# Two transformer blocks on one core: the last mixer by pairs of heads, another order of its projections, and other fillings of the pauses

## The chip, the core and the metric

The kernel runs on one of the eight cores of a Trainium2 chip. Five engines work side by side and meet at semaphores: TensorE (PE, matrix products), VectorE (DVE), ScalarE (ACT), GpSimd (POOL) and SyncE (SP, which issues the transfers here). The metric is device time in microseconds; lower is better. Three runs of the kernel before took 1088.26, 1089.15 and 1089.99 us.

## The reference, cut to what matters

One sequence of 256 tokens of width 1024 goes through three layers: a first block (gated delta rule and attention as mixer 1, then an MLP) and two layers of a second block: mixer 2 (differential attention) with MLP, and mixer 3 (stick-breaking attention) with MLP. Everything is float32. The change is about mixer 3:

```python
def stick_breaking_attention(h, w_q, w_o, k, v):      # 16 heads of 64
    q = (h @ w_q).reshape(b, s, B_HEADS, B_HEAD_DIM).transpose(0, 2, 1, 3)
    def block(args):
        qb, start = args
        z = jnp.einsum('bhqd,bhkd->bhqk', qb, k).astype(f32) * scale
        mask = kpos[None, :] < qpos[:, None]
        log_beta = jax.nn.log_sigmoid(z)
        log_1m = jnp.where(mask, jax.nn.log_sigmoid(-z), 0.0)
        between = lax.cumsum(log_1m, axis=3, reverse=True) - log_1m
        a = jnp.where(mask, jnp.exp(log_beta + between), 0.0)
        return jnp.einsum('bhqk,bhkd->bqhd', a.astype(v.dtype), v)
    ...
    return o @ w_o
# around it, for each layer: x = x + rms_norm(mixer(rms_norm(x))), x = x + rms_norm(swiglu(rms_norm(x)))
```

k and v come from `rms_norm(x) @ kv_w` with a gain of their own.

## The kernel before, in words

**Weights.** All weights stream through the same path. `raws` lists them in the order of use; each is one transfer of 1 MB into one of three `RAW` buffers and two "halves" of 128x1024. ACT copies a half, rounded, to `WH` (L1393) and DVE subtracts to get the rest, `WL` (L1839); in mixer 3 every other subtraction is POOL's (L2419). A product of float32 quality is then three matmuls, high by high, low by high, high by low (`mm3`, L653 to L655). A half lies in one of eight slots: slots 0 to 3 are `WH`/`WL`, slots 4 to 7 are `SPARE`, a region that overlaps the scratch of the mixers and so belongs to the MLPs alone. `ahead(n)` in ACT's, DVE's and POOL's programs prepares all halves up to n+3, and a half waits until PE is done with the one that held its slot before.

**Order.** Nothing is scheduled at run time. Each engine runs its own program in order, and `in_order` makes all of them follow the same written list of steps (`STAGE_4` for mixer 3), each engine taking from it the steps that it has a function for. Each entry below is a step: `p.j` is projection half j, 24 in all, in the order of `S_ORDER` (v, k and q, four pieces each, two halves a piece); `o.i` multiplies by half i of the output weight.

**Mixer 3 before.** Step `s.h` of head h has three parts on PE. For h-4 it forms the sums (`b_sums`): two products of a triangle of ones and one of a full square of ones with the softplus of the scores, which gives the reverse cumulative sum, 128x256, 128x128 and 128x128 (L1365 to L1367). For h it forms the scores (`b_score`), keys by queries, with 64 rows of the array (L1354, L1355: 256 and 128 columns, since the mask leaves out a quarter). For h-6 it forms the values (`b_values`), whose output is 64 partitions high (L1377, L1378). Even heads use rows or columns 0 to 63 of the array, odd heads 64 to 127. All of these operands are plain float32, and each of these matmuls runs as two passes. Between them DVE scales and masks (L2381), ACT takes the absolute value and the exponential, then for four heads at once (`l.p`) the logarithm, DVE completes the softplus (L2389), adds the sums (L2376), and ACT takes the last exponential. The buffers ZM and LS hold eight heads of 128x384 each. The values of a pair of heads go to `MH`/`ML` as soon as the last key or value projection has read these (until then to `OT`), since the projections of k and v read their input there, and those of q read `UH`/`UL`.

**Output.** Steps o.0 to o.5 add one half of the output weight each to four tiles of 128x512 in PSUM. `out_last` (o.6) takes the last two halves tile by tile, so that tile (0,0) ends first.

**Between stages.** `between(r)` is the work of ACT, DVE and POOL from the finished sums to the next input: squares (`sq`), gain (`mx`), root on POOL (`r0`, `r1`), addition to H (`ad`), squares of H (`hs`), scaling (`xn`, L1855), then 16 pieces of features (`fe`), each transposed by PE (L687), scaled by ACT and DVE. r = 1, 3, 5 stand behind the three mixers, 2, 4, 6 behind the three MLPs. PE waits in `entry(r)`: it runs `WARM[r]` dummy products first (`keep_warm`, L664), then four transposes, then transposes and first products in turn. After mixer 1 (`BETWEEN_FIRST`) the preparation of the MLP's halves is spread over this work (`hi.k`, `lo.k`); after mixers 2 and 3 it all stands before or behind it.

## Time and profile before

| | us |
|---|---|
| median of three runs | 1089.15 (1088.26 to 1089.99) |
| the profiled execution, its own time | 1094.96 |
| span in it, first to last instruction | 1093.1 |
| PE busy | 1048.6 (96%) |
| PE weight loads busy | 953.5 (87%) |
| DVE busy | 637.7 (58%) |
| ACT busy | 563.2 (52%) |
| POOL busy | 85.2 (8%) |

All times in views are microseconds from the start of the span. Matmuls are pipelined, so the ends of PE's rows are modelled; the distance from the start of one row to the start of the next is what a piece of work takes on PE, and the text uses that. An idle time and what ended it stand in brackets behind a row. PEclk is the granted clock, 1.00 being 2.4 GHz. Mixer 3 runs from about 747 to 891, the last MLP from 903 to 1083.

### The profile page before, as it was taken

What the parts mean: (1) busy time and instruction counts of PE and PEld (TensorE: products, weight loads), DVE (VectorE), ACT (ScalarE), POOL (GpSimd) and SP (SyncE); (2) the same over time, 40 slices, a digit from 0 to 9 for tenths busy, and PEclk for the clock granted to TensorE, in tenths of its full rate; (3) what the DMA queues carried; (4) which work ended last, traced back from release to release, by engine and by line L of the source; (5) the groups of instructions that cost most, each with busy time, mean ns of one, the idle gap of its engine ahead of it and who ended that gap; (6) DMA issues with size and microseconds to landing.
All of it is one profiled execution on the core that took longest, in us unless ns stands there. A gap on an engine that the chain in (4) does not pass through costs nothing.

```text
span 1093.1 us, 17642 instructions
## 1 busy us (share of the span) xinstructions
PE 1048.6 (96%) x7367; PEld 953.5 (87%) x7367; DVE 637.7 (58%) x984; ACT 563.2 (52%) x1009; POOL 85.2 (8%) x84
## 2 busy tenths in 40 slices
PE   6999899999999999999899999998999999999997
PEld 5989887889999887988789999997999879999996
DVE  4797644587464557677875545548344566454553
ACT  5662354466453546556464434437676656343442
POOL 3012010110000001000100000000322210000000
PEclk9999899999999999999999999999999999999999
DMA  8323111074556454433346556464433334654641
GB/s 263 116 78 93 62 40 40 1 229 152 198 168 216 157 213 152 155 116 117 116 136 231 173 174 228 143 207 136 155 116 117 116 103 155 225 172 175 226 145 54
DMA packets 114974, 160.34 MB, mean 147 GB/s; under 512 B 3776, under 2 KB 99264, under 8 KB 114896
## 3 DMA queue, kind: packets, MB, share of 16 engines
q1 hardware_dynamic: 114896, 159.22, 43.8%
q8 instruction: 58, 0.95, 0.4%
q14 instruction: 20, 0.16, 0.0%
HBM read 158.16 MB, written 1.05 MB: 146 GB/s over the span
## 4 chain that ended last, share of the span: by engine, by line
PE 83%; DVE 9%; ACT 4%; issue 2%; POOL 1%; DMA 0%; SPq 0%; DVEq 0%; POOLq 0%; ACTq 0%
PE PS L653 23%; PE PS L655 22%; PE PS L654 22%; ACT SCR L1393 2%; DVE WL L1839 2%; PE PS L982 1%; PE PS L1354 1%; POOL SM L2423 1%; PE PS L687 1%; DVE SPARE L1839 1%; PE PS L1377 1%; PE PS L1275 1%; PE PS L977 1%; PE PS L1365 1%; DVE H L1875 1%
## 5 line engine op out<-in xcount | busy, mean ns | idle before, releaser
L1839 DVE TENSOR_TENSOR WL<-RAW,WH 128x1024 fp32r<-128x1024 f32 (+1 forms) x177 | 213.9, 1234 | 71.6 <-ACT WH L1393 71.4
L1393 ACT ACTIVATE WH<-RAW 128x1024 fp32r<-128x1024 f32 (+1 forms) x191 | 195.1, 1049 | 46.6 <-DMA RAW<-in_gu 28.9
L653 PE MATMUL PS<-UH,WH 128*128 128x256 f32 (+2 forms) x680 | 195.7, 288 | 3.9 <-DVE WL L1839 3.0
L655 PE MATMUL PS<-UH,WL 128*128 128x256 f32 (+2 forms) x680 | 194.4, 286 | 0.0
L654 PE MATMUL PS<-UL,WH 128*128 128x256 f32 (+2 forms) x680 | 194.4, 286 | 0.0
L1393 ACT ACTIVATE SCR<-PS 128x512 f32<-128x512 f32 (+7 forms) x233 | 100.7, 468 | 171.2 <-PE PS L655 118.9
L653 PEld LDWEIGHTS PS<-UH,WH 128*128 128x128 f32 (+1 forms) x680 | 129.8, 191 | 6.4 <-DVE WL L1839 3.7
L1839 DVE TENSOR_TENSOR SPARE<-RAW,SPARE 128x1024 fp32r<-128x1024 f32 x100 | 118.0, 1219 | 22.1 <-ACT SPARE L1393 22.1
L654 PEld LDWEIGHTS PS<-UL,WH 128*128 128x128 f32 (+1 forms) x680 | 129.3, 190 | 1.1
L655 PEld LDWEIGHTS PS<-UH,WL 128*128 128x128 f32 (+1 forms) x680 | 129.8, 191 | 0.5
L1937 DVE TENSOR_TENSOR SCR<-SCR,PS 128x512 f32<-128x512 f32 x34 | 23.4, 687 | 159.4 <-PE PS L655 108.2
L1393 ACT ACTIVATE SPARE<-RAW 128x1024 fp32r<-128x1024 f32 x100 | 100.3, 1048 | 27.3 <-DMA RAW<-in_gu 20.7
L653 PE MATMUL PS<-WH,MH 128*128 128x512 f32 (+1 forms) x288 | 108.3, 376 | 2.4 <-DVE ML L2395 1.2
L654 PE MATMUL PS<-UL,SPARE 128*128 128x256 f32 x384 | 108.2, 282 | 0.0
L653 PE MATMUL PS<-UH,SPARE 128*128 128x256 f32 x384 | 108.1, 281 | 0.0
L655 PE MATMUL PS<-UH,SPARE 128*128 128x256 f32 x384 | 107.6, 280 | 0.0
L654 PE MATMUL PS<-WL,MH 128*128 128x512 f32 (+1 forms) x288 | 105.4, 366 | 0.0
L655 PE MATMUL PS<-WH,ML 128*128 128x512 f32 (+1 forms) x288 | 105.3, 366 | 0.0
L2423 POOL TENSOR_TENSOR SM<-SM 128x1 f32<-128x1 f32 (+5 forms) x32 | 26.8, 840 | 778.4 <-DVE SM L1850 623.3
L1393 ACT ACTIVATE MH<-SCR 128x512 fp32r<-128x512 f32 (+1 forms) x37 | 22.6, 615 | 124.0 <-DVE SCR L1937 124.0
L653 PE MATMUL PS<-WH,UH 128*128 128x256 f32 (+2 forms) x264 | 80.9, 306 | 0.1
L654 PE MATMUL PS<-WL,UH 128*128 128x256 f32 (+2 forms) x264 | 76.5, 290 | 0.0
(307 smaller groups left out, 2093.2 us busy)
## 6 DMA issues: line engine op xcount, KB each, us to landing
RAW<-in_gu SPq DMA_DIRECT2D x44, 1024.0 KB, 5.3
RAW<-in_dn SPq DMA_DIRECT2D x22, 1024.0 KB, 7.2
RAW<-in_w_up SPq DMA_DIRECT2D x16, 1024.0 KB, 6.2
RAW<-in_w_down SPq DMA_DIRECT2D x16, 1024.0 KB, 5.0
RAW<-in_a_qkv SPq DMA_DIRECT2D x12, 1024.0 KB, 5.1
RAW<-in_w_in SPq DMA_DIRECT2D x11, 1024.0 KB, 5.3
RAW<-in_kv_w SPq DMA_DIRECT2D x8, 1024.0 KB, 5.6
RAW<-in_w_out SPq DMA_DIRECT2D x4, 1024.0 KB, 4.9
```

Source lines behind the costliest of these rows:

```text
L653: e.matmul(o, lh, rh, start=start, stop=False)
L654: e.matmul(o, lh, rl, start=False, stop=False)
L655: return e.matmul(o, ll, rh, start=False, stop=stop)
L687: e.transpose(PS[:, b, o:o + 128], XN[:, c, 128 * k:128 * k + 128], idn).then_inc(*turned.step((r, c, k)))
L977: ins = e.matmul(v[:, h, :], MT[:, h, :], X[:, h, :], start=True, stop=True)
L982: ins = e.matmul(v[:, h, :], XT[:, h, :], T0[:, h, :], start=True, stop=True)
L1275: ins = e.matmul(PS[:, 4 + i, 0:nk], QTT[64 * i:64 * i + 64, h, 128 * c:128 * c + 128], KTT[64 * i:64 * i + 64, h, 0:nk], start=True, stop ...
L1354: e.matmul(PS[:, b, 0:256], KTS[hp:hp + 64, j, 0:128], QTS[hp:hp + 64, j, :], start=True, stop=True)
L1393: return e.activation(o, i, func, bias=bias, scale=scale, accum_out=acc)
L1839: e.tensor_tensor(lo_of(n_), half_src(n_), hi_of(n_).bitcast(F32), SUB).then_inc(s_lo_dve, 1)
L1937: e.tensor_tensor(FB[:, g % 2, 1, :], FB[:, g % 2, 0, :], PS[:, ub + ((g - begun) * nb + nb - 1) % 4, :], MUL).then_inc(*f_2.step((r, g)))
L2423: e.tensor_tensor(o, x, s, POW).then_inc(*done)
```

## The change

It has four parts.

1. Mixer 3 works on pairs of heads q = 0 to 7. A step s.q makes the scores of both heads, head by head in turn, so that neighbouring matmuls lie in rows 0 to 63 and 64 to 127 of the array, in two PSUM banks. A new step c.q makes the sums of both heads (one matmul of 384 columns in place of 256 and 128, and one of 128), and a new step u.q the values of both, in columns 0 to 63 and 64 to 127 of the array and in the two halves of the partitions of one PSUM bank. The elementwise operations between are 128x768 instead of twice 128x384, and `l.p` (ACT) and the new `t.p` (DVE) take two pairs.
2. The projections come in another order: q1 before v1, q2 before v2, q3 before k3 and v3. The mixer's result goes to `UH`/`UL`, free once q3 is projected, instead of `MH`/`ML`. Four halves of the output weight instead of two are taken tile by tile at the end (`out_last`); steps o.4 and o.5 go.
3. The first MLP halves after mixers 2 and 3 lie in slots 4 to 7 first, as they did after mixer 1, and `BETWEEN_FIRST`, renamed `BETWEEN_MLP`, is used after all three mixers.
4. `WARM` changes, and three more dummies stand behind the first four transposes of every `entry`.

```diff
-S_ORDER = "v0 k0 q0 k1 v1 q1 k2 v2 q2 k3 v3 q3".split()
+S_ORDER = "v0 k0 q0 k1 q1 v1 k2 q2 v2 q3 k3 v3".split()
 STAGE_4 = steps_of(
-    "p.0 p.1 p.2 p.3 p.4 p.5 s.0 p.6 s.1 p.7 s.2 p.8 s.3 p.9 l.0 p.10 p.11 s.4 p.12 s.5 p.13 s.6 p.14 s.7 p.15 l.1 "
-    "p.16 p.17 s.8 p.18 s.9 p.19 s.10 p.20 s.11 p.21 l.2 p.22 os.0 p.23 s.12 os.1 o.0 s.13 o.1 s.14 o.2 s.15 o.3 l.3 "
-    "o.4 s.16 s.17 o.5 s.18 s.19 sv.14 sv.15 o.6")
+    "p.0 p.1 p.2 p.3 p.4 p.5 s.0 p.6 s.1 p.7 l.0 t.0 p.8 p.9 c.0 p.10 s.2 u.0 p.11 c.1 p.12 s.3 u.1 p.13 l.1 t.1 p.14 "
+    "c.2 p.15 s.4 u.2 p.16 c.3 p.17 s.5 u.3 p.18 l.2 t.2 p.19 p.20 c.4 p.21 s.6 u.4 os.0 p.22 s.7 os.1 p.23 p.24 c.5 l.3 "
+    "t.3 o.0 u.5 o.1 c.6 o.2 c.7 o.3 u.6 u.7 o.6")
-WARM = {0: 14, 1: 2, 2: 2, 3: 18, 4: 2, 5: 18}
+WARM = {0: 14, 1: 6, 2: 4, 3: 17, 4: 7, 5: 3}
...
-                head = (4, 5, 6, 7, 0, 1, 2, 3) if r == 2 else (0, 1, 4, 5, 2, 3, 6, 7, 4, 5)
+                head = (4, 5, 6, 7, 0, 1, 2, 3, 4, 5)[:8 + (b - a) % 8]
...
                 for k in range(4):
                     turn(0, k)
+                keep_warm(3, SUMS[r])
...
-                        out_last(r, [half_of(("out", r, 3), j) for j in range(2)], [6, 7], [mix_ready(r, 6), mix_ready(r, 7)])
+                        ks = range(4 if r == 5 else 6, 8)
+                        out_last(r, [half_of(("out", r, k // 2), k % 2) for k in ks], ks, [mix_ready(r, k) for k in ks])
...
+            def b_score(q):
+                ...
+                for kt in range(2):
+                    for i in range(2):
+                        hp = slice(64 * i, 64 * i + 64)
+                        ins = e.matmul(PS[:, i, 256 * kt:256 + 128 * kt], KTS[hp, q, 128 * kt:128 * kt + 128], QTS[hp, q, 128 * kt:],
+                                       start=True, stop=True)
+            def b_sums(q):
+                pe.wait_ge(*sh_sp[q])
+                for i in range(2):
+                    l = LS[q % 4][:, i, :]
+                    pe.wait_ge(*emptied[i])
+                    e.matmul(PS[:, i, 0:384], C["inclb"], l, start=True, stop=False)
+                    ins = e.matmul(PS[:, i, 128:256], C["ones"], l[:, 256:384], start=False, stop=True)
+            def b_values(q):
+                b, w = 2 + q % 2, LS[q % 4]
+                ...
+                for kt in range(2):
+                    for i in range(2):
+                        h = 2 * q + i
+                        ins = e.matmul(PS[64 * i:64 * i + 64, b, 128 * kt:256], VS[:, kt, 64 * h:64 * h + 64], w[:, i, 256 * kt:256 + 128 * kt],
+                                       start=kt == 0, stop=kt == 1)
...
-                in_order({1: BETWEEN_FIRST, 6: BETWEEN_LAST}.get(r, BETWEEN), dict(sq=sq, hs=hs, xn=xn, fe=fe, hi=next_halves))
+                in_order(BETWEEN_LAST if r == 6 else BETWEEN_MLP if r + 1 in MLP else BETWEEN, dict(sq=sq, hs=hs, xn=xn, fe=fe, hi=next_halves))
...
-                return lambda i: ahead(half_of(("out", r, i // 2), i % 2) if i < 6 else LAST_OUT[r] + 1)
+                return lambda i: ahead(half_of(("out", r, i // 2), i % 2) if i < 6 else LAST_OUT[r])
+                return lambda i: ahead(half_of(("out", r, i // 2), i % 2) if i < 6 else LAST_OUT[r] - 1)
```

In the last three lines the first is ACT's and DVE's before, the second ACT's now, the third DVE's now.

How the instructions move, at three places. (A row is line, operation, output and inputs, shape of the output; x2 means twice in a row.) First PE in the middle of mixer 3, where before every block between two projection halves holds the sums, scores and values of one head each:

```order
L1365 MATMUL PS<-SCR,CST 128x256
L1366 MATMUL PS<-SCR,CST 128x128
L1367 MATMUL PS<-SCR,CST 128x128
L1354 MATMUL PS<-SCR 128x256
L1355 MATMUL PS<-SCR 128x128
L1377 MATMUL PS<-SCR 64x256
L1378 MATMUL PS<-SCR 64x128
```

The same place of the changed kernel, a block of sums, then, 24 projection matmuls later, a block of scores and values:

```order
L1372 MATMUL PS<-SCR,CST 128x384
L1373 MATMUL PS<-SCR,CST 128x128
L1372 MATMUL PS<-SCR,CST 128x384
L1373 MATMUL PS<-SCR,CST 128x128
...
L1361 MATMUL PS<-SCR 128x256 x2
L1361 MATMUL PS<-SCR 128x128 x2
L1387 MATMUL PS<-SCR 64x256 x2
L1387 MATMUL PS<-SCR 64x128 x2
```

Scores and values of the two heads of a pair now stand next to each other, and the sums stand alone in their blocks.

Second, DVE at the end of mixer 3 and the start of the work behind it, before (L2376 adds the sums, L2395 and L2401 split the result, L1839 is a half's low part, L1869 `mx`, L1850 `r0` or `r1`, L1875 `ad`):

```order
L2376 SCALAR_TENSOR_TENSOR SCR<-PS,SCR 128x384 [waits s_bsum] x2
L2395 SCALAR_TENSOR_TENSOR ML<-PS,MH 128x256 [waits s_mix_hi] x2
L1839 TENSOR_TENSOR WL<-RAW,WH 128x1024 [waits s_hi]
L1839 TENSOR_TENSOR SPARE<-RAW,SPARE 128x1024 [waits s_hi] x2
L1869 SCALAR_TENSOR_TENSOR SCR<-PS,WROW 128x512 [waits s_wrow,s_mixsq0]
L1850 TENSOR_SCALAR SM<-SM 128x1 [waits s_mixsq0]
L1869 SCALAR_TENSOR_TENSOR SCR<-PS,WROW 128x512
L1875 SCALAR_TENSOR_TENSOR H<-SCR,SM,H 128x512 [waits s_mixed0,s_root0]
```

and now (the same operations are L2393, L2398, L1845, L1879, L1856 and L1885):

```order
L2393 SCALAR_TENSOR_TENSOR SCR<-PS,SCR 128x768 [waits s_bsum] x2
L1845 TENSOR_TENSOR WL<-RAW,WH 128x1024 [waits s_hi]
L2398 SCALAR_TENSOR_TENSOR UL<-PS,UH 128x256 [waits s_mix_hi] x2
L1845 TENSOR_TENSOR SPARE<-RAW,SPARE 128x1024 [waits s_hi] x2
L1879 SCALAR_TENSOR_TENSOR SCR<-PS,WROW 128x512 [waits s_wrow,s_mixsq0]
L1845 TENSOR_TENSOR SPARE<-RAW,SPARE 128x1024 [waits s_hi]
L1856 TENSOR_SCALAR SM<-SM 128x1 [waits s_mixsq0]
L1879 SCALAR_TENSOR_TENSOR SCR<-PS,WROW 128x512
L1885 SCALAR_TENSOR_TENSOR H<-SCR,SM,H 128x512 [waits s_mixed0,s_root0]
```

One subtraction for the next MLP has moved from before the first `mx` to behind it, ahead of `r0`.

Third, ACT around the second logarithm (SCR<-SCR,SM with the constant one as bias), now; before, its place had four operations of 128x384 and three projection halves before the next sums:

```order
L1402 ACTIVATE SCR<-SCR 128x768 [waits s_bz]
L1402 ACTIVATE SCR<-SCR 128x768 [waits s_bexp]
L1402 ACTIVATE SCR<-PS 128x256 [waits s_bvalue]
L1402 ACTIVATE WH<-RAW 128x1024 [waits s_raw0]
L1402 ACTIVATE SCR<-PS 128x256 [waits s_half]
L1402 ACT_TABLE_LOAD
L1402 ACTIVATE SCR<-SCR,SM 128x768
L1402 ACTIVATE SCR<-SCR,SM 128x768 [waits s_bexp]
```

These eight stand between the scores s.3 and the sums c.2, while PE's list has two projection halves (p.13, p.14) there.

## Rows read from the trace of the kernel before

**Rows 1.** Mixer 3 as one window: busy times and counts by engine, PEclk, DMA share, GB/s.
```profile
773.00:886.00 113.00, 111.37 (x730) 97.35 (x729) 46.95 (x67) 76.56 (x126) 28.51 (x12) 1.00 0.36 121
```
**Rows 2.** PE's waits at 905 to 915: in total, times, longest (565 to 580 reads the same).
```profile
PE PS L653 <- DVE WL L1839: 0.8, 1, 0.8
```
**Rows 3.** Timeline of PE, one block of mixer 3 and one half: start, busy, instruction, count.
```profile
803.84 0.59 PE L1365 MATMUL PS<-SCR,CST 128*128 128x256 f32 x2
804.81 0.70 PE L1354 MATMUL PS<-SCR 64*128 64x256 f32 x2
805.66 0.65 PE L1377 MATMUL PS<-SCR 128*64 128x256 f32 x2
806.45 0.39 PE L653 MATMUL PS<-WH,MH 128*128 128x256 f32 x1
...
809.43 0.59 PE L1365 MATMUL PS<-SCR,CST 128*128 128x256 f32 x2
```
**Rows 4.** Timeline of PE, the last two blocks of mixer 3.
```profile
873.29 0.38 PE L1365 MATMUL PS<-SCR,CST 128*128 128x256 f32 x1
...
878.22 0.47 PE L653 MATMUL PS<-WH,MH 128*128 128x512 f32 x1 [1.23 <-DVE ML L2395]
...
881.06 0.38 PE L1365 MATMUL PS<-SCR,CST 128*128 128x256 f32 x1
...
886.00 0.47 PE L653 MATMUL PS<-WH,MH 128*128 128x512 f32 x1
```
**Rows 5.** Timeline of PE in mixer 2: scores of two heads in opposite row halves.
```profile
452.26 0.70 PE L1275 MATMUL PS<-SCR 64*128 64x256 f32 x4
452.89 0.38 PE L653 MATMUL PS<-WH,UH 128*128 128x256 f32 x1
```
**Rows 6.** Timeline of PE in mixer 3: values of heads 13 and 14, then of 15.
```profile
883.90 0.66 PE L1377 MATMUL PS<-SCR 128*64 128x256 f32 x4
...
885.17 0.65 PE L1377 MATMUL PS<-SCR 128*64 128x256 f32 x2 [0.40 <-ACT SCR L1393]
```
**Rows 7.** Timeline of PE in mixer 1: both column halves into one bank.
```profile
141.41 0.28 PE L1121 MATMUL PS<-CST,SCR 128*64 128x128 f32 x1
141.62 0.43 PE L1122 MATMUL PS<-CST,SCR 128*64 128x128 f32 x2
```
**Rows 8.** Groups of 757 to 892 by shape: busy, mean ns, idle before.
```profile
L1393 ACT ACTIVATE WH<-RAW 128x1024 fp32r<-128x1024 f32 x30 | 31.7, 1055 | 0.0
L1393 ACT ACTIVATE SCR<-SCR 128x384 f32<-128x384 f32 x48 | 25.0, 525 | 32.4 <-DVE SCR L2376 24.6 <-DVE SCR L2381 7.2
L1393 ACT ACT_TABLE_LOAD x9 | 11.5, 1283 | 0.2
...
L1839 DVE TENSOR_TENSOR WL<-RAW,WH 128x1024 fp32r<-128x1024 f32 x16 | 22.8, 1425 | 24.0 <-ACT WH L1393 24.0
L2376 DVE SCALAR_TENSOR_TENSOR SCR<-PS,SCR 128x384 f32<-128x384 f32 x16 | 8.9, 555 | 26.0 <-PE PS L1367 25.9
L1839 DVE TENSOR_TENSOR SPARE<-RAW,SPARE 128x1024 fp32r<-128x1024 f32 x2 | 2.4, 1218 | 0.0
...
L2419 POOL TENSOR_TENSOR WL<-RAW,WH 128x1024 fp32r<-128x1024 f32 x14 | 33.5, 2394 | 86.9 <-ACT WH L1393 86.9
```
**Rows 9.** Timeline of PE, the pause behind mixer 3.
```profile
891.56 4.18 PE L664 MATMUL PS<-CST 128*128 128x128 f32 x36
...
897.47 0.36 PE L653 MATMUL PS<-WH,UH 128*128 128x256 f32 x1
```
**Rows 10.** Timeline of PE, the pause behind mixer 1.
```profile
236.79 0.60 PE L664 MATMUL PS<-CST 128*128 128x128 f32 x4
238.19 0.66 PE L687 MATMUL PS<-CST,SCR 128*128 128x128 f32 x4 [0.80 <-DVE SCR L1855]
239.46 0.30 PE L687 MATMUL PS<-CST,SCR 128*128 128x128 f32 x1 [0.61 <-DVE UL L1888]
239.62 0.36 PE L653 MATMUL PS<-SPARE,UH 128*128 128x256 f32 x1
```

More of the change, by code:

```diff
@@ new lines, in b_log, with b_sums, b_values @@
+            def b_log(p):
+                for q in (2 * p, 2 * p + 1):
+                    l = LS[q % 4]
+                    ac.wait_ge(*sh_x[q, "exp"])
+                    act(l, l, ACT.Ln, bias=ONEC).then_inc(*sh_l.step(q))
+            def b_sums(q):
+                ac.wait_ge(*sh_zz[q])
+                act(LS[q % 4], ZM[q % 4], ACT.Exp).then_inc(*sh_a.step(q))
+            def b_values(q):
+                ac.wait_ge(*sh_u[q])
+                if q < 4:
+                    act(OT[:, q, :], PS[:, 2 + q % 2, 0:256], ACT.Copy).then_inc(*sh_o.step(q))
+                else:
+                    ac.wait_ge(s_half, Q_LAST + 1)
+                    act(UH[:, q, 16:], PS[:, 2 + q % 2, 0:256], ACT.Copy).then_inc(*mx_hi.step((5, q)))
@@ L1865, in between, with next_halves @@
             def between(r):
+                def next_halves(k):
+                    ahead(LAST_OUT[r] + 1 + k, 0)
                 def mx(c, i):
```

198 lines of the change are left out of this document (79 added, 119 removed).

## The prediction

> **What bounds the kernel now.** I read three views, in this order. The windows by stage first: from 773 to 886, in mixer 3, PE is busy 111.4 of 113.0 us at a granted clock of 1.00, ACT 76.6, DVE 47.0, POOL 28.5 [rows 1]. The reader should see that PE's list itself is the bound there. Then PE's waits: around the start of the last MLP there is one wait of 0.8 us for a half's low part, and the same at 565 to 580 behind mixer 2 [rows 2]; in mixer 3 the waits are 1.23 us for a split result and 0.40 us for an exponential, both near the end [rows 4, 6]. Then PE's timeline, from start to start: where does its time go that is not projection? So what PE no longer has to do in mixer 3 comes off the time one for one, until the elementwise engines become late.
>
> **The mixer's blocks on PE.** Between two projection halves stands a block of plain float32 products. In one full block [rows 3] the sums of a head take 804.81 - 803.84 = 0.97 us, its scores 805.66 - 804.81 = 0.85, its values 806.45 - 805.66 = 0.79, together 2.61; one half after it 809.43 - 806.45 = 2.98. By the order of steps the kernel before has 18 blocks: 4 of scores alone (3.4), 2 of sums and scores (2 x 1.82 = 3.6), 10 full ones (26.1), and the last two, 878.22 - 873.29 = 4.93 and 886.00 - 881.06 = 4.94 [rows 4], with the waits in them. The sum is 43.0 us.
>
> The changed kernel has 18 blocks too, of other content: 3 of scores, 5 of scores and values, 8 of sums, one of values of one pair and one of two. What a pair costs depends on whether matmuls in opposite halves of the array run together. Two rows show it. In mixer 2, two heads' scores of 256 columns (x4: two heads by two passes) take 452.89 - 452.26 = 0.63 us from start to start [rows 5]; one head's 256 and 128 columns take 0.85, so two heads one after the other with 256 columns would be near 1.1. And in mixer 3 the values of heads 13 and 14, which happen to be neighbours, show 0.66 us busy for x4 where head 15 alone shows 0.65 for x2 [rows 6]. So I take scores of a pair at the price of one head, 0.85, and values of a pair at 0.79. Sums use the whole array and gain nothing from pairing: 2 x 0.97 = 1.94, less a change of operand (384 columns in one matmul), 1.9. Then: 3 x 0.85 = 2.6; 5 x 1.64 = 8.2; 8 x 1.9 = 15.2; values alone about 0.85 and 1.5. The sum is 28.3, **14.7 us less**. The number of halves and blocks stays, so what surrounds them stays.
>
> **New waits in the mixer.** A pair goes through DVE, ACT (three times), DVE, PE, DVE, ACT in 768 columns. ACT's 384 columns take 0.525 and 1024 take 1.055, so 768 take about 0.84; DVE's 0.555 for 384 and 1.22 for 1024 give 0.95 [rows 8]. That is less than two narrow operations (1.05 and 1.11), so no engine gets more work. But the way to the first sums of a batch is longer. At the second logarithm, with T the start of s.3 on PE: the scaled scores are there at T+1.9, absolute value and exponential end at T+3.6, then ACT, in its order, copies a result (0.4), prepares a half (1.06), copies a projection (0.4), loads the table (1.28) and takes the logarithm (0.84), T+7.6; DVE's softplus ends at T+8.55. PE reaches c.2 after scores, values and only two halves, T + 1.64 + 2 x 2.95 = T+7.5. PE waits **1.1 us**. What is queued behind c.2 on PE is p.15 and s.4, which nobody else hurries for. At the other three batches the same count leaves room: c.0 and c.4 have three halves before them (1.1 to 1.9 us to spare), c.6 has p.23, c.5, o.0, u.5 and o.1 (1.6 to spare). The values wait for sums, DVE 0.95 and ACT 0.84; a half and the next scores, 3.8 us, cover that. From none to four waits of this kind: 0 to 4 us.
>
> At the end, the last output half (k=7) can only be prepared by ACT behind the last two values: copy 0.4, cast 1.06, then POOL 2.39 [rows 8], 3.9 us; meanwhile PE has 15 products of (891.56 - 886.00)/24 = 0.232 us [rows 4, 9], 3.5 us. **0.5 us** of wait, 0 to 1.
>
> **The pause behind mixer 3.** From the end of the output products to the first product of the MLP it is now 897.47 - 891.56 = 5.9 us, 4.2 of them dummies [rows 9]. Behind mixer 1, where four halves are already taken tile by tile, so that 24 products stand behind the end of tile (0,1) and not 12, it is 239.62 - 236.79 = 2.8 [rows 10]. The changed kernel does the same behind mixer 3: **3.1 us less** (12 x 0.232 = 2.8 from the products alone; 2.5 to 3.6).
>
> **The other halves.** Behind mixers 2 and 3 the halves n+4 and n+5 are now prepared among the last features, as after mixer 1. That takes away the wait of 0.8 us at both places [rows 2]: **1.6 us less** (1.0 to 2.2). Behind mixer 2 there are still two halves at the end, so its pause of some 5.9 us stays; one subtraction (1.22) now stands ahead of the first root and another ahead of `r1`, against two fewer ahead of the first `mx`: **0.2 us more** (-0.5 to +0.7).
>
> **The dummies.** A dummy is two passes, 4.18 us for 36 [rows 9], 0.11 each beyond the latency of the last. Behind mixer 1 four more dummies make 0.9 us against an idle 0.80, and the three new ones 0.65 against an idle 0.61 [rows 10]. They fill the idle time to the brim and PE then starts late by a tenth at most places: **0.3 us more** over five pauses (0 to 0.8). They can only give something back through the clock, and these windows already read 1.00; I count nothing.
>
> **The sum:** -14.7 + 1.1 + 0.5 - 3.1 - 1.6 + 0.2 + 0.3 = -17.3 us. The profiled execution took 1094.96, which gives 1077.7; its own time is 0.5% above the median of the runs, 1089.15, and on their scale it is 1089.15 - 17.3 = **1071.9 us**.
>
> **A rule weighed.** The two matmuls of a pair's values will write the same PSUM bank, in different partitions. The rows for values in opposite halves [rows 6] are of heads 13 and 14, which write two banks. The only place that writes both column halves of one bank in turn is in mixer 1, where the second starts 141.62 - 141.41 = 0.21 us after the first [rows 7], no overlap for 128 columns; but there the first is a transpose and the second a product, which may be the reason. The Trainium skill says (TensorEngine Tiling (Array Packing), Restrictions and Gotchas) that tiles of different rows cannot access one PSUM bank at the same time. It speaks of row tiles; by it the scores, in two banks, are safe, and if it held for column tiles too, the values would give nothing.
>
> **Rivals.**
> - *Values serialize in their bank.* For it: rows 7. Against it: both halves have partitions of their own. Each pair then pays a second stream of 384 columns in two passes, 0.85 - 0.21 = 0.64 us: 8 x 0.64 = 5.1 us back, 1077.0.
> - *The elementwise chain is later than I count.* DVE's subtractions take 1.43 us in the mean where POOL works at the same time, 1.22 where it doesn't [rows 8]. If wide DVE operations suffer too (0.95 more on each of the two before the sums) and ACT's are no shorter than two narrow ones (0.2 more on each of three), every batch is 2.5 us later: c.2 waits 3.6, c.0 and c.6 about 1 each, 4 us more than in the sum, 1075.9. The Trainium skill (the same page, Performance Considerations) warns that packing speeds up TensorE and not the emptying of PSUM; here that would show as this case.
> - *No overlap at all*, scores and values both: 10.2 us back, 1082.1. Rows 5 and 6 speak against it.
> - *Slower than before: the clock.* With half of the array idle in every score and value block and new waits beside them, PE might be granted 1.2 GHz in parts of mixer 3. A stretch at that level costs half its length, so the gain is gone once about 35 of the mixer's 105 us run at it; 40 us would give 1091.9 less rounding, 1092. For it: nothing in mixer 3 itself; against it: the clock reads 1.00 there with 64-row products and the same 18 blocks [rows 1], and the changed blocks are shorter.
>
> **Chances.** The forecast 0.68, with its own range 1069 to 1074.5; the late chain 0.13; values serialized 0.10; no overlap 0.04; the clock 0.05. The range that holds 8 in 10 takes in the first three: 1068 to 1079 (the lower end is no new wait, 1.6 us, and the better bounds of the pause and the halves). A change of 0.2% (2.2 us) is about what a measurement of this kernel can tell from none. All cases but the clock lie beyond it: faster 0.94, the same 0.02, slower 0.04.
>
> **What would show it.** In the profile after: a block of scores and values of a pair at about 1.65 us from start to start, and scores alone at 0.85 (if 1.5, no overlap; if the values part is 1.4, the bank); sums of a pair at 1.9; PE waiting for the softplus once, about 1 us, at c.2 and hardly at c.0, c.4, c.6; the pause behind mixer 3 at 2.8 us with its transposes right behind the dummies; no wait for a low part at the start of the second and third MLP; PEclk at 1.00 in mixer 3; everything up to 545 as before. The forecast is wrong if mixer 3 with its pause is less than 13 us shorter, or if time comes or goes outside of it by more than 3 us, which nothing here accounts for.

## The result, and the profile after

The changed kernel takes **1070.38 us** (median of four runs, 1069.62 to 1071.47) against 1089.57 for the kernel before: a ratio of 0.982 with a 95% interval of 0.980 to 0.984, that is 19.2 us less. Measured again beside the last experiments (after_again), it was 1069.17 us against 1089.02 (0.981, 0.979 to 0.983). The forecast was 1071.9.

The profiled execution took 1069.62 us, with a span of 1067.8. That is 25 us less than the profiled execution of before, more than the medians differ, because TensorE was granted half its clock in four stretches there (17 us in all, around 21, 129, 151 and 489 us) and in one here (3.4 us, around 482), not counting the last few us of both. Such stretches come and go between executions of one kernel (after_again has none of them), so I compare stage by stage.

**Mixer 3 as a window** (columns as in [rows 1]), from the first score block to the end of the output products:

```profile
766.00:870.50 104.50, 103.32 (x723) 88.84 (x722) 49.57 (x53) 77.01 (x109) 29.63 (x14) 1.00 0.44 141
```

PE is still the engine that is almost never idle: 103.3 of 104.5 us at a clock of 1.00. Before, the same work went from 773.02 to 891.56, 118.54 us; now from 766.06 to 870.47, 104.41: **14.1 us less**. ACT's and DVE's busy time has not shrunk (77.0 and 49.6 us against 76.6 and 47.0 [rows 1], where the window leaves out the last output products), but the window is shorter, so ACT now works 74% of it.

**PE's timeline, the blocks**, in the place of [rows 3]:

```profile
766.06 0.92 PE L1361 MATMUL PS<-SCR 64*128 64x256 f32 x8
766.91 0.39 PE L652 MATMUL PS<-MH,WH 128*128 128x256 f32 x1
...
779.49 0.81 PE L1372 MATMUL PS<-SCR,CST 128*128 128x384 f32 x2
...
781.00 0.38 PE L1373 MATMUL PS<-SCR,CST 128*128 128x128 f32 x2
781.14 0.36 PE L652 MATMUL PS<-WH,MH 128*128 128x256 f32 x1
...
784.18 0.92 PE L1361 MATMUL PS<-SCR 64*128 64x256 f32 x8
785.04 0.87 PE L1387 MATMUL PS<-SCR 128*64 128x256 f32 x8
785.84 0.39 PE L652 MATMUL PS<-WH,MH 128*128 128x256 f32 x1
```

Read from start to start: the scores of two heads (x8: two heads, two key tiles, two passes) take 766.91 - 766.06 = 0.85 us, what one head took before; scores and values of a pair 785.84 - 784.18 = 1.66; the sums of a pair 781.14 - 779.49 = 1.65, where I had put 1.9.

**The wait at the sums of pair 2**, PE first, then what ACT did in the meantime:

```profile
802.00 0.91 PE L1372 MATMUL PS<-SCR,CST 128*128 128x384 f32 x2 [0.88 <-DVE SCR L2388]
```

```profile
795.46 1.73 ACT L1402 ACTIVATE SCR<-SCR 128x768 f32<-128x768 f32 x2 [1.12 <-DVE SCR L2382]
797.10 0.36 ACT L1402 ACTIVATE SCR<-PS 128x256 f32<-128x256 f32 x1
797.36 1.05 ACT L1402 ACTIVATE WH<-RAW 128x1024 fp32r<-128x1024 f32 x1
798.32 0.39 ACT L1402 ACTIVATE SCR<-PS 128x256 f32<-128x256 f32 x1
798.73 1.28 ACT L1402 ACT_TABLE_LOAD   x1
800.02 1.76 ACT L1402 ACTIVATE SCR<-SCR,SM 128x768 f32<-128x768 f32 x2
```

The reader should see the half (WH, 1.05 us) and two copies between the exponential and the logarithm. The two halves before this block take 6.85 us instead of the 5.82 of e8, where nothing is waited for: a wait of 1.0. Only one other block of sums waits, and shortly: at the sums of pair 7 the output half before them and they themselves take 3.05 and 1.73 us, where e2, whose value blocks are longer, has 2.84 and 1.65. That is 0.3 us; the view of waits does not list it. DVE is adding the sums of pair 6 just then (851.53 to 852.47, the sums of pair 7 start at 852.62), late behind a subtraction of 2.30 us.

**The end of mixer 3 and the pause**, in the place of [rows 4, 9]:

```profile
857.29 1.52 PE L1387 MATMUL PS<-SCR 128*64 128x256 f32 x16
858.74 0.50 PE L652 MATMUL PS<-WH,UH 128*128 128x512 f32 x1
...
862.73 0.50 PE L652 MATMUL PS<-WH,UH 128*128 128x512 f32 x1 [0.25 <-POOL WL L2422]
...
870.47 0.83 PE L663 MATMUL PS<-CST 128*128 128x128 f32 x6
871.68 0.66 PE L686 MATMUL PS<-CST,SCR 128*128 128x128 f32 x4 [0.39 <-DVE SCR L1861]
...
873.07 0.36 PE L652 MATMUL PS<-SPARE,UH 128*128 128x256 f32 x1
```

The last 48 products take 11.73 us where 48 x 0.232 would be 11.1; the rest is the wait for POOL's low part. The pause is 873.07 - 870.47 = 2.60 us (5.91 before). In the MLPs behind mixers 2 and 3, the first 78 products behind the last transpose take 9.62 and 9.61 us (10.35 and 10.39 before), and the waits of [rows 2] are gone. The pause behind mixer 2 is 5.80 (5.91), and its transposes wait for DVE, not for the dummies:

```profile
551.43 0.66 PE L686 MATMUL PS<-CST,SCR 128*128 128x128 f32 x4 [0.45 <-DVE SCR L1861]
```

**The groups** of 757 to 872 that answer to [rows 8]:

```profile
L1402 ACT ACTIVATE SCR<-SCR 128x768 f32<-128x768 f32 x24 | 20.3, 845 | 22.9 <-DVE SCR L2393 12.7 <-DVE SCR L2382 10.0
L2382 DVE SCALAR_TENSOR_TENSOR SCR<-PS,CST 128x768 f32<-128x768 f32 x8 | 7.6, 956 | 8.9 <-PE PS L1361 8.9
```

Twice as wide costs ACT 845 ns against 525 and DVE 956 against 555, the 0.84 and 0.95 that I had interpolated.

### The profile page after: what moved, and what is told of

Read it like the earlier page. It is cut to its first block, busy times and chain, and to the rows that moved or that the text cites. A ratio compares the mean times of both kernels' runs of the same rounds, so it can differ in the third digit from the quotient of the medians.

```text
span 1067.8 us, 17553 instructions
## 1 busy us (share of the span) xinstructions
PE 1030.7 (97%) x7355; PEld 937.9 (88%) x7355; DVE 633.2 (59%) x960; ACT 557.2 (52%) x978; POOL 85.5 (8%) x84
## 3 DMA queue, kind: packets, MB, share of 16 engines
HBM read 158.16 MB, written 1.05 MB: 149 GB/s over the span
## 4 chain that ended last, share of the span: by engine, by line
PE 86%; DVE 8%; ACT 3%; issue 2%; POOL 1%; DMA 0%; SPq 0%; DVEq 0%; POOLq 0%; ACTq 0%
PE PS L652 24%; PE PS L654 23%; PE PS L653 23%; ACT SCR L1402 2%; PE PS L985 1%; DVE WL L1845 1%; PE PS L1372 1%; PE PS L686 1%; PE PS L663 1%; POOL SM L2426 1%; PE PS L1278 1%; PE PS L980 1%; PE PS L1361 1%; DVE SCR L2002 1%; DVE H L1885 1%
## 5 line engine op out<-in xcount | busy, mean ns | idle before, releaser
L1845 DVE TENSOR_TENSOR WL<-RAW,WH 128x1024 fp32r<-128x1024 f32 (+1 forms) x177 | 214.1, 1235 | 66.6 <-ACT WH L1402 66.4
L652 PE MATMUL PS<-UH,WH 128*128 128x256 f32 (+2 forms) x712 | 202.3, 284 | 2.4 <-DVE WL L1845 1.3
L654 PE MATMUL PS<-UH,WL 128*128 128x256 f32 (+2 forms) x712 | 200.9, 282 | 0.0
L653 PE MATMUL PS<-UL,WH 128*128 128x256 f32 (+2 forms) x712 | 200.7, 282 | 0.0
L1845 DVE TENSOR_TENSOR SPARE<-RAW,SPARE 128x1024 fp32r<-128x1024 f32 x100 | 119.5, 1233 | 25.0 <-ACT SPARE L1402 25.0
L653 PEld LDWEIGHTS PS<-UL,WH 128*128 128x128 f32 (+1 forms) x712 | 133.3, 187 | 0.9
L653 PE MATMUL PS<-UL,SPARE 128*128 128x256 f32 x352 | 99.2, 282 | 0.0
L652 PE MATMUL PS<-UH,SPARE 128*128 128x256 f32 x352 | 98.9, 281 | 0.0
L654 PE MATMUL PS<-UH,SPARE 128*128 128x256 f32 x352 | 98.6, 280 | 0.0
L652 PE MATMUL PS<-WH,MH 128*128 128x512 f32 (+1 forms) x256 | 95.1, 371 | 1.1 <-DVE ML L2230 1.0
L653 PE MATMUL PS<-WL,MH 128*128 128x512 f32 (+1 forms) x256 | 92.9, 363 | 0.0
L654 PE MATMUL PS<-WH,ML 128*128 128x512 f32 (+1 forms) x256 | 92.8, 363 | 0.0
L1402 ACT ACTIVATE MH<-SCR 128x512 fp32r<-128x512 f32 x34 | 21.5, 633 | 126.5 <-DVE SCR L1943 126.5
```

Of the source, the lines that this page charges most:

```text
L652: e.matmul(o, lh, rh, start=start, stop=False)
L653: e.matmul(o, lh, rl, start=False, stop=False)
L654: return e.matmul(o, ll, rh, start=False, stop=stop)
L1402: return e.activation(o, i, func, bias=bias, scale=scale, accum_out=acc)
L1845: e.tensor_tensor(lo_of(n_), half_src(n_), hi_of(n_).bitcast(F32), SUB).then_inc(s_lo_dve, 1)
```

## The experiments

Each is the changed kernel with one edit, so its time is to be held against 1070.4 us (and 1069.2, the second measurement). The medians of one kernel lie 1 to 1.5 us apart; where an edit is worth less, the stretch of the profile that it touches decides.

### Do the two heads overlap because of the halves? (e1, e2)

```diff
-                        hp = slice(64 * i, 64 * i + 64)
+                        hp = slice(0, 64)
```

> The changed kernel, but both heads of a pair multiply their scores with keys and queries of partitions 0 to 63, so all four score products of a pair lie in one half of the array (the second head's scores are computed from the first head's operands, so that part of the result is another). Theory A (the two heads of a pair overlap because they lie in opposite halves): the second head's 384 columns in two passes no longer lie beside the first's; a pass of 384 columns took 0.323 us in the sums, so a score block alone grows from 0.85 to about 1.49 us and the eight pairs cost 8 x 0.64 = 5.1 us: 1070.4 -> about 1075.5 us. Rival B (the blocks are short because a pair is issued as one group with one wait, whatever the halves): a score block stays at 0.85 us and the kernel at 1070.4 us.

Measured: 1075.34 us (0.987 of before, 0.985 to 0.990), 5.0 more than the changed kernel. PE's timeline:

```profile
766.64 1.57 PE L1361 MATMUL PS<-SCR 64*128 64x256 f32 x8
768.14 0.39 PE L652 MATMUL PS<-MH,WH 128*128 128x256 f32 x1
```

The same x8 now take 1.50 us instead of 0.85, in all eight blocks. Theory A holds to 0.01 us, B is out.

```diff
-                        ins = e.matmul(PS[64 * i:64 * i + 64, b, 128 * kt:256], VS[...], w[...], start=kt == 0, stop=kt == 1)
+                        ins = e.matmul(PS[0:64, b, 256 * i + 128 * kt:256 * i + 256], VS[...], w[...], start=kt == i == 0, stop=kt == i == 1)
```

> The changed kernel, but the value products of both heads of a pair write PSUM partitions 0 to 63 (the second head into columns 256 to 511 of the same bank, which nothing reads, so the second head's values are missing from the result). Theory A (the heads overlap across the halves, although they write one bank): a value block alone grows from 0.80 to about 1.44 us, the pair of blocks u.6 u.7 from 1.45 to about 2.75, and the eight pairs cost 8 x 0.64 = 5.1 us: 1070.4 -> about 1075.5 us. Rival B (products that write the same bank go one after the other in the changed kernel already, so nothing is left to lose): value blocks stay at 0.80 us and the kernel at 1070.4 us.

Measured: 1074.01 us (0.985, 0.984 to 0.987), 3.6 more. PE's timeline, the values in a block of scores and values, and the block of two pairs' values:

```profile
785.65 1.51 PE L1387 MATMUL PS<-SCR 128*64 128x256 f32 x8
787.09 0.39 PE L652 MATMUL PS<-WH,MH 128*128 128x256 f32 x1
...
861.52 2.81 PE L1387 MATMUL PS<-SCR 128*64 128x256 f32 x16
864.26 0.50 PE L652 MATMUL PS<-WH,UH 128*128 128x512 f32 x1
```

The values take 1.44 us instead of 0.80, and 2.74 instead of 1.45. The blocks sum to the 5.1 us of theory A (8 x 0.64). From the first scores to the end of the output products the profile is 4.9 us longer (109.34 against 104.41). The median shows 3.6 of it, with intervals wide enough for both. So in the changed kernel the two heads' values do run side by side although they write one bank: the rival of the serial bank is refuted, and each pair is worth 0.64 us here.

### Must the halves alternate in program order? (e3)

```diff
-                for kt in range(2):
-                    for i in range(2):
+                for i in range(2):
+                    for kt in range(2):
```
(in the scores and in the values)

> The changed kernel, but the four score products of a pair, and its four value products, stand head by head (first head's two, then the second's two) instead of alternating between the halves of the array. Theory A (products overlap only with their direct neighbour in program order: a product waits for its own half, and what stands behind it waits too): the first head's 128-column product and the second head's 256-column product still overlap, nothing else does; a score block is 0.43 + 0.64 + 0.2 = about 1.28 us instead of 0.85, a value block 1.23 instead of 0.80, and 16 blocks cost 16 x 0.43 = 6.8 us: about 1077 us. Rival B (the array finds the other half's work in any order): no change, 1070.4 us. Rival C (no overlap at all without alternation): blocks of 1.49 and 1.44 us, +10.2 us: about 1080.6 us.

Measured: 1070.64 us (0.982, 0.980 to 0.984). PE's timeline:

```profile
785.59 0.93 PE L1361 MATMUL PS<-SCR 64*128 64x256 f32 x8
786.45 0.88 PE L1387 MATMUL PS<-SCR 128*64 128x256 f32 x8
787.26 0.39 PE L652 MATMUL PS<-WH,MH 128*128 128x256 f32 x1
```

1.67 us for the block, as if nothing had been changed; only the block of two pairs' values is a little longer, 1.50 us instead of 1.45. Theory A was wrong, B right: with all of the first head's products ahead in the program, the second head's first one starts 14 ns after the first head's (785.604 and 785.590); with the halves in turn it was 7 ns. For blocks of this size it is enough that the other half's work stands in the same block. In the trace the four records of 256 columns come first, then the four of 128, so the second head's product started before one that stands ahead of it in the kernel's text. How far ahead this reaches was not tried.

### Why the sums took 1.65 us and not 1.9 (e4, e9)

```diff
-                    e.matmul(PS[:, i, 0:384], C["inclb"], l, start=True, stop=False)
-                    ins = e.matmul(PS[:, i, 128:256], C["ones"], l[:, 256:384], start=False, stop=True)
+                    e.matmul(PS[:, i, 0:256], C["inclb"], l[:, 0:256], start=True, stop=False)
+                    e.matmul(PS[:, i, 128:256], C["ones"], l[:, 256:384], start=False, stop=True)
+                    ins = e.matmul(PS[:, i, 256:384], C["inclb"], l[:, 256:384], start=True, stop=True)
```

> The changed kernel, but each head's running sums are three products again (256, 128 and 128 columns) as in the kernel before, instead of one of 384 and one of 128. The block of a pair's sums took 1.65 us where I had taken 1.9. Theory A (it is short because it stands alone between products that use the whole array, so no change between half and whole array lies in it; the joined product is worth nothing, since the columns are the same): the block stays at 1.65 us, to within 0.05, and the kernel at 1070.4 us. Rival B (joining the 256 and the 128 columns saved the missing 0.25 us): blocks of 1.9 us, 8 x 0.25 = +2.0 us: 1072.4 us.

Measured: 1069.56 us (0.981, 0.980 to 0.983). PE's timeline:

```profile
778.99 0.59 PE L1372 MATMUL PS<-SCR,CST 128*128 128x256 f32 x2
...
779.64 0.39 PE L1374 MATMUL PS<-SCR,CST 128*128 128x128 f32 x2
779.87 0.60 PE L1372 MATMUL PS<-SCR,CST 128*128 128x256 f32 x2
...
780.52 0.39 PE L1374 MATMUL PS<-SCR,CST 128*128 128x128 f32 x2
780.66 0.36 PE L652 MATMUL PS<-WH,MH 128*128 128x256 f32 x1
```

1.67 us: one matmul in place of two is worth 0.02 us. B is out. What stays is the place of the block, and for that the block was put in front of values again:

```diff
-    "... c.0 p.10 s.2 u.0 p.11 c.1 p.12 s.3 u.1 p.13 l.1 t.1 p.14 "
-    "c.2 p.15 s.4 u.2 p.16 c.3 p.17 s.5 u.3 ..."
+    "... c.0 p.10 s.2 p.11 c.1 u.0 p.12 s.3 p.13 u.1 l.1 t.1 p.14 "
+    "c.2 p.15 s.4 p.16 c.3 u.2 p.17 s.5 u.3 ..."
```
(as the line shows, the values of pair 1 also moved behind a half, away from the scores; no sums stand next to them)

> The changed kernel with two value blocks moved: those of pairs 0 and 2 stand right behind the sums of pairs 1 and 3 instead of behind the scores of pairs 2 and 4 (two projection halves each change places with them). Theory A (in the kernel before, every block of sums was followed by products that use half of the array, which start some 0.12 us later than a product that uses the whole array would; in the changed kernel the sums stand alone, and this is the 0.25 us per pair by which they came in under my 1.9): the two blocks of sums take about 1.77 us from their start to the first value product, against 1.65 for the others, the value products 0.80, and nothing else changes: 1070.4 to 1070.7 us. Rival B (the sums are short for another reason, what stands behind them does not matter): both stay at 1.65 us.

Measured: 1069.59 us (two runs; 0.981, 0.979 to 0.984). PE's timeline:

```profile
787.01 0.81 PE L1372 MATMUL PS<-SCR,CST 128*128 128x384 f32 x2
...
788.52 0.39 PE L1373 MATMUL PS<-SCR,CST 128*128 128x128 f32 x2
788.84 0.87 PE L1387 MATMUL PS<-SCR 128*64 128x256 f32 x8
```

From the start of the sums to the first value product it is 788.84 - 787.01 = 1.83 us, and the same in the other moved block: 0.18 more than 1.65, where theory A had 0.12 (1.77); rival B is out. The values behind take 0.80 as forecast. The last group of sums is followed 788.84 - 788.52 = 0.32 us later by the half-array products, and in the changed kernel 781.14 - 781.00 = 0.14 later by a product over the whole array. With that the old price can be rebuilt. In the kernel before, every head's sums stood before half-array products and ended in the same way (its last group started at 804.49, the scores at 804.81: 0.32). Two heads: 1.67 as in e4, less its two tails (779.87 - 779.64 = 0.23 and 0.14), plus 2 x 0.32, is 1.94, which is the 2 x 0.97 of [rows 3]. So the missing 0.25 to 0.3 us was a change from the whole to half of the array that no longer falls behind sums.

### The last four halves tile by tile (e5)

```diff
-    "... o.2 c.7 o.3 u.6 u.7 o.6"
+    "... o.2 c.7 o.3 u.6 u.7 o.4 o.5 o.6"
-                        ks = range(4 if r == 5 else 6, 8)
+                        ks = range(6, 8)
-WARM = {0: 14, 1: 6, 2: 4, 3: 17, 4: 7, 5: 3}
+WARM = {0: 14, 1: 6, 2: 4, 3: 17, 4: 7, 5: 17}
```

> The changed kernel, but only the last two halves of mixer 3's output go tile by tile, as in the kernel before (halves 4 and 5 go over all four tiles ahead of them), with 17 dummies in the pause. Theory A (the pause is what the products left behind the first two summed tiles do not cover; each half more in the tile-by-tile part adds 6 products of 0.232 us behind them): the pause behind mixer 3 grows from 2.60 back to about 5.8 us; the 0.6 us wait for the low part of the last half may go, since more products then stand ahead of it: +2.6 to +3.2 us in all, 1070.4 -> about 1073.3 us. Rival B (the pause is short because other work of mixer 3, the pairs' element operations, leaves the engines free at that moment): the pause stays at 2.6 us and the kernel at 1070.4 us.

Measured: 1072.66 us (0.985, 0.982 to 0.987). PE's timeline, the pause:

```profile
870.78 3.96 PE L663 MATMUL PS<-CST 128*128 128x128 f32 x34
875.17 0.66 PE L686 MATMUL PS<-CST,SCR 128*128 128x128 f32 x4 [0.43 <-DVE SCR L1861]
...
876.56 0.35 PE L652 MATMUL PS<-SPARE,UH 128*128 128x256 f32 x1
```

The pause is 5.78 us, 3.2 more; the last 48 products take 11.18, 0.55 less, because the wait for the last half's low part is gone. The edit costs 2.6 in the profile and 2.3 in the median: theory A. Both numbers of the prediction, 3.1 and 0.5, are borne out, and they belong together: the 0.5 is the price of the 3.1. The transposes still wait for DVE (0.43 us), so it is not the 34 dummy passes that make the pause long.

### Preparing the MLP's halves early (e6)

```diff
-                in_order(BETWEEN_LAST if r == 6 else BETWEEN_MLP if r + 1 in MLP else BETWEEN, ...)
+                in_order(BETWEEN_LAST if r == 6 else BETWEEN_MLP if r == 1 else BETWEEN, ...)
-                return lambda i: ahead(... if i < 6 else LAST_OUT[r])        # ScalarE; VectorE: LAST_OUT[r] - 1
+                return lambda i: ahead(... if i < 6 else LAST_OUT[r] + 1)
```

> The changed kernel, but the halves that the MLP behind mixers 2 and 3 needs first are prepared in the order of the kernel before (up to the fourth at the end of the mixer's output on ScalarE and VectorE, the next ones only in the MLP). Theory A (each MLP then waits 0.8 us for the low part of its fifth and sixth half): the first 78 products of each of these MLPs grow from about 9.6 back to 10.4 us, 2 x 0.8 = +1.6 us: 1070.4 -> 1072.0 us. Rival B (the wait went because mixer 3's end is quicker or the pause shorter, so behind mixer 2 at least nothing comes back from this edit): both stay at 9.6 us and the kernel at 1070.4 us. The two pauses should stay at 5.8 and 2.6 us, to within 0.3.

Measured: 1070.71 us (0.983, 0.981 to 0.984). PE's waits at 560 to 572; 882 to 893 reads the same:

```profile
PE PS L652 <- DVE WL L1845: 0.8, 1, 0.8
```

The 78 products take 10.37 and 10.38 us: A's 2 x 0.76 came back. But the pauses moved, which I had not expected. Behind mixer 2 it is 5.22 instead of 5.80, behind mixer 3 3.24 instead of 2.60. PE's timeline of the first:

```profile
546.14 3.96 PE L663 MATMUL PS<-CST 128*128 128x128 f32 x34
549.93 0.60 PE L686 MATMUL PS<-CST,SCR 128*128 128x128 f32 x4
...
551.36 0.36 PE L652 MATMUL PS<-SPARE,UH 128*128 128x256 f32 x1
```

Here nothing is waited for at the transposes: their input is ready while the 34 dummy passes (17 dummies) still run. DVE starts the first scaling 2.86 us after the start of the pause (549.00), and 3.88 in the changed kernel (550.90), where a subtraction of 1.22 us stands ahead of each of two roots. So the early preparation costs 1.0 us of this chain and 0.6 of the pause; the dummies hide the rest. Behind mixer 3 it is the other way round: with all four subtractions ahead of the first `mx` (6.0 us of DVE), that one starts at 866.32, 3.38 us before the pause; with two there (3.7 us) it starts at 864.82, 5.65 us before it. That takes 0.6 off the pause; over both it is worth the 1.6 us of the forecast (-1.52 - 0.64 + 0.58), which the median neither shows nor excludes (0.3 and 1.5 above the two measurements of the changed kernel).

### What the dummies do (e7, e11)

```diff
-WARM = {0: 14, 1: 6, 2: 4, 3: 17, 4: 7, 5: 3}
+WARM = {0: 14, 1: 2, 2: 2, 3: 18, 4: 2, 5: 0}
-                keep_warm(3, SUMS[r])
```

> The changed kernel with the dummies of the kernel before in all pauses but the one behind mixer 3 (2, 2, 18, 2 products ahead of the turns instead of 6, 4, 17, 7, none behind mixer 3, and not the 3 between the turns and the first products). Theory A (at a granted clock of 1.00 in and behind all pauses, dummies that end before the awaited data cost nothing and bring nothing): all pauses keep their lengths to within 0.05 us, the clock behind them stays at 1.00, and the kernel stays at 1070.4 us. Rival B (the added dummies keep the clock up: without them TensorE's granted clock falls to one half for some stretch behind a pause): +3 to +5 us for each such stretch, visible as a granted clock under 1.00 right behind a pause. Rival C (the dummies delay the first products): -0.3 us at each of five pauses, about 1068.9 us.

Measured: 1073.22 us (0.984, 0.983 to 0.986), 2.8 more than the changed kernel. The four pauses that have dummies keep their lengths (2.80, 2.55, 5.81, 3.20), so C is out. But right behind the pause of mixer 3 the window reads (1.00 on both sides of it):

```profile
877.00:880.50 3.50, 3.50 (x19) 3.50 (x18) 2.58 (x9) 2.33 (x8) 0.54 (x1) 0.51 0.83 202
```

The granted clock is 0.51 for 3.5 us. So A is wrong, and B has the right kind of cost. Idle time in a pause is not enough for it, though. The pause behind the second MLP has more of it in this same profile, with two dummies (four passes) ahead of it, and the clock behind it reads 1.00, as it does behind the same pause of the kernel before:

```profile
746.72 0.66 PE L686 MATMUL PS<-CST,SCR 128*128 128x128 f32 x4 [1.21 <-DVE SCR L1860]
```

One execution could be chance, so the pause behind mixer 3 alone was stripped:

```diff
-WARM = {..., 5: 3}
+WARM = {..., 5: 0}
-                keep_warm(3, SUMS[r])
+                keep_warm(0 if r == 5 else 3, SUMS[r])
```

> The changed kernel without any dummies in the pause behind mixer 3 (the other pauses keep theirs). In the run with the old dummies TensorE's granted clock fell to one half for 3.4 us right behind this pause, and the six products at 877 us took 1.38 us instead of 0.79. Theory A (the dummies keep the clock up here): a stretch of half clock right behind this pause again, 1.2 to 1.5 us more in the profile's products, about 1071.8 us. Rival B (that stretch fell there by chance, as such stretches fall elsewhere in some executions): clock 1.00 behind the pause, pause of 2.6 us with or without dummies, 1070.4 us.

Measured: 1073.46 us (1067.77 to 1073.72; 0.983, 0.981 to 0.986), 4.3 above after_again, which ran beside it. PE's timeline of the pause, and then the window behind it:

```profile
871.61 0.66 PE L686 MATMUL PS<-CST,SCR 128*128 128x128 f32 x4 [1.05 <-DVE SCR L1861]
872.87 0.30 PE L686 MATMUL PS<-CST,SCR 128*128 128x128 f32 x1 [0.61 <-DVE UL L1898]
...
873.31 0.42 PE L654 MATMUL PS<-SPARE,UL 128*128 128x256 f32 x1
```

```profile
873.00:877.00 4.00, 4.00 (x23) 4.00 (x22) 3.41 (x10) 2.32 (x8) 0.25 (x1) 0.57 0.66 143
```

The same stretch again, in both profiles without dummies there and in none of the eleven profiles of the changed kernel and its variants with them. Each matmul record grows from 0.28 to 0.42 us, and from the last value block to the end of the MLP's first 78 products it takes 35.94 us instead of 34.68: 1.26 us. The median says more, 2.8 to 4.3 us. In three of e11's five runs the clock over the whole span is 0.993, in its profiled run 0.996, so there may be further such stretches, but only the profiled run shows where they lie. The fifth run, at 0.998, took 1067.77 us, no more than the changed kernel at its best (1067.59), so the stretch need not come every time. A is right in kind; how often the stretch comes, and where the rest of the median comes from, stays open. Fewer than six dummies, but more than none, were not tried there.

### Towards a better version (e8, e10)

```diff
-    "... p.12 s.3 u.1 p.13 l.1 t.1 p.14 " ... "c.7 o.3 u.6 u.7 o.6"
+    "... p.12 s.3 l.1 t.1 u.1 p.13 p.14 " ... "c.7 o.3 k.0 u.6 u.7 o.6"
+    (ScalarE only:) k=lambda _: ahead(LAST_OUT[5] - AHEAD)
```

> The changed kernel with two steps of mixer 3 moved. The logarithms of pairs 2 and 3 (and the maximum on VectorE) stand right behind the scores of pair 3, ahead of the copy of pair 1's values and of the preparation of a weight half on ScalarE; and ScalarE prepares the last half of the output ahead of its copies of pairs 6 and 7, not behind them. Theory A (the sums of pair 2 wait 1.0 us because ScalarE prepares a half, 1.05 us, ahead of the logarithms; the last 48 products wait 0.6 us because the low part of the last half is taken off late on GpSimd for the same reason): the 48 products ahead of the sums of pair 2 take 5.85 us instead of 6.85, the last 48 take 11.15 to 11.3 instead of 11.73: -1.5 us, 1070.4 -> 1068.9 us. Rival B (other waits stand right behind these two, the copies that are now later or the next half's preparation): each wait comes back within the next two blocks, and the kernel stays at 1070.4 us.

Measured: 1070.64 us (1068.16 to 1073.39; 0.982, 0.980 to 0.984). PE's timeline at the sums of pair 2:

```profile
803.93 0.81 PE L1372 MATMUL PS<-SCR,CST 128*128 128x384 f32 x2
```

No wait stands there any more, nor at the transposes of the pause. The 48 products before these sums take 5.82 us (6.85), the last 48 take 11.23 (11.73), the pause 2.23 (2.60); from the first scores to the end of the MLP's first 78 products it is 123.96 us against 125.91, 1.95 less, and PE's view of waits is empty there. (The short wait before the sums of pair 7 stays.) Theory A holds in the profile. The median does not show it, as this profile has half-clock stretches in mixer 1 and a longer one at the start, which the changed kernel's has not.

```diff
+                    if (r, i) == (3, 5):
+                        return
-                        ks = range(4 if r == 5 else 6, 8)
+                        ks = range({3: 5, 5: 4}[r], 8)
```
(on top of the two moves)

> The changed kernel with the two moves in mixer 3 of the run before (logarithms of pairs 2 and 3 right behind the scores of pair 3; the last half of the output prepared ahead of the copies of pairs 6 and 7), and the fifth half (of 0 to 7) of mixer 2's output goes tile by tile with the last two. Theory A: mixer 3 from its first score block to the end of the MLP's first 78 products is 1.95 us shorter, as it was in the run before; 6 products of 0.232 us more stand behind the first two summed tiles of mixer 2, so the pause behind it shrinks from 5.80 to about 4.4 us: -3.3 us, 1070.4 -> about 1067.1 us. Rival B (with one half less ahead of it, the products of the last two halves wait for the heads' copies, and the pause's gain is lost again): mixer 2 as a whole stays as it is, 1068.5 us.

Measured beside the changed kernel (after_again, below): **1066.68 us** (1065.52 to 1072.62; 0.979, 0.977 to 0.982) against 1069.17, 2.5 less. Mixer 3 keeps its gain (123.88 us). The pause behind mixer 2 shrinks only to 5.13, and the timeline says why, PE first, then DVE:

```profile
546.81 3.96 PE L663 MATMUL PS<-CST 128*128 128x128 f32 x34
550.60 0.60 PE L686 MATMUL PS<-CST,SCR 128*128 128x128 f32 x4
...
551.81 0.30 PE L686 MATMUL PS<-CST,SCR 128*128 128x128 f32 x1
```

```profile
549.23 0.48 DVE L1863 TENSOR_SCALAR SCR<-H,SM 128x512 f32<-128x512 f32 x1
```

The transposes wait for nothing: the pause is as long as its own dummies and transposes. DVE starts their input 2.42 us into the pause, 1.46 earlier than the 3.88 of the changed kernel, which is the whole 1.4 of theory A; the 34 dummy passes end only at 3.79 us, and 0.7 is left. Neither theory had that. The 0.7 is not lost again inside mixer 2: from the first product behind the first MLP's pause to the end of this one it is 134.16 us, and 134.85 in e11, whose profile has a half-clock stretch at the same place (518). So B is out. Fewer dummies there were not tried. It is the fastest version here, by its median and its lowest run (1065.52); the intervals of the two ratios overlap, so it is the profile that says where the 2.6 us are.

> The changed kernel once more, unchanged, beside the next three on the same chip: 1070.4 us by the runs so far (1069.6 to 1071.5). It says how far two measurements of one kernel lie apart, against which differences of 1 to 3 us are to be read.

Measured: 1069.17 us (1067.59 to 1070.05), 1.2 under the first measurement. Its profile has no half-clock stretch at all before its last 1 us.

## Why the prediction was right

Against the steps of the sum, in its order:

- **The blocks**: forecast 43.0 to 28.3 us. Adding up the 18 blocks of the profile after gives 3 x 0.85 + 5 x 1.65 + 6 x 1.65 + 1.76 + 1.73 + 0.80 + 1.45 = 26.4, **16.6 less, not 14.7**. Scores and values came out as forecast (e1 and e2 show that it is the halves). The mis-sized term is the sums, 13.4 instead of 15.2: I took their price from a place where half-array products stood behind them (e4, e9). Of the 16.6 us 2.4 come back elsewhere: the 528 projection and output products between the blocks took 75.6 us before and take 77.9. Of that, 1.6 are the two waits below and 0.2 the one before the sums of pair 7, which was not in the sum at all; the other 0.5 are halves with other neighbours (a projection half directly before scores or values takes 3.04 us where it takes 2.97 before sums). "The number of halves and blocks stays, so what surrounds them stays" is the sentence that failed there.
- **The wait at c.2**: forecast 1.1, measured 1.0, at that place and for that reason (e8 removes it by moving the half). The first sums of the other batches do not wait.
- **The last half**: forecast 0.5 (its own 3.9 - 3.5 makes 0.4), measured 0.6 (e5 and e8 take 0.5 of it away).
- **The pause behind mixer 3**: forecast 5.9 to 2.8, measured 2.60; e5 gives it back.
- **The fifth and sixth halves**: forecast -1.6. The products got 0.73 and 0.78 us shorter; e6 puts both back, and shows that 0.6 is moved from one pause to the other.
- **The pause behind mixer 2**: forecast +0.2, measured -0.1. That this came out small is partly luck: two larger effects meet in it. The two subtractions ahead of the roots make the chain 1.0 us longer (e6). The new slots shorten it by 1.1: from the start of the pause to the first scaling it was 3.98 us before (557.08), and it is 2.86 in e6, which keeps the new slots and has the old order. I had counted 0.2 for the first, net of the two subtractions fewer ahead of `mx`, and nothing for the second.
- **The dummies**: forecast +0.3 and "count nothing" for the clock. The pauses did not get longer (0.1 less over the other three). The nothing came out as a number, since neither kernel has a half-clock stretch behind a mixer's pause, but the view behind it failed: without the six dummies behind mixer 3 such a stretch stood there in two of two profiles, 1.3 us in the profile and more in the medians. I had judged them by a profile whose pause was filled with 36 passes; in the shortened pause the question is what happens without them, which no row of before could show.

The stages of the two profiles add up: mixer 3 -14.1, its pause -3.3, the two MLP starts -1.5, the other pauses -0.2, in all **-19.1 us**, and the medians differ by 19.2. Forecast was -17.3; the 1.8 between them are 1.8 for the sums and 0.9 for the dummies and pauses, less the 0.7 at the halves, and some tenths of rounding. So the total is this close partly because errors of either sign cancel. The Trainium skill (TensorEngine Tiling (Array Packing), Restrictions and Gotchas) bars one bank to tiles of different rows only; e2 shows for column tiles that they share a bank without loss, so the rival built on [rows 7] was priced rightly (5.1) and did not happen. The late chain did not happen either: DVE's wide operations take 956 ns in the mean, not twice 0.95. I had said that everything up to 545 would be as before, and in the profiles it is 6.1 us shorter; that is the clock of one execution, since after_again and the first profile of the same kernel differ there by 2.1 us.

## What to carry to other kernels

Where products of two heads that need only half of the array's rows or columns stand in one block, put them in opposite halves and expect the second head free; price each kind of block by what stands behind it, since a change from the whole array to half of it costs 0.07 us (behind projections) to 0.18 (behind sums) here. When a pause is shortened, look again at its dummies from both sides: too many become the pause (e6, e10), none at all can cost the clock behind it (e7, e11). When a chain is reordered, look at where it is ready and not only at PE's pause, since dummies hide what was gained. And a gain of 1 to 2 us in 1070 is read from its stretch of the profile, not from a median.

## What the runs showed of the hardware that I had not expected

- Products in opposite column halves write one PSUM bank at the same time: 4 x 2 matmul records of two heads in 0.80 us, the time of one head (after), and 1.44 when both use one half (e2).
- The two halves start 7 ns apart with alternating program order and 14 ns apart with all of one half's four products first; the block's time is the same (1.66 us in the changed kernel and 1.67 in e3).
- Behind the start of the last whole-array group of the sums (float32, 128 columns, two passes), a half-array product starts 0.32 us later (e9), a whole-array product 0.14 (after).
- A pause of 2.6 us with idle gaps of 1.05 and 0.61 us and no dummies in it was followed by 3.4 us at half clock in two of two profiles (e7, e11); with dummies in it, in none of eleven. A pause of 3.2 us elsewhere, with idle gaps of 1.21 and 0.61 us and four dummy passes, was not followed by one (before, e7).
